# Loading a page of cached values as 64 partitions of two neighbouring rows

## The reference, cut to what matters

```python
PAST_LEN = 4096; PAGE_SIZE = 128; N_HEADS = 8; HEAD_DIM = 64; DEC_BATCH = 8; DEC_SEQ = 8
...
    past = cache_k[layer, page_table[:, :cb * ppb]].astype(f32)      # all 32 pages of each sequence
    kmean = past.reshape(B, cb, MOBA_BLOCK, N_HEADS, HEAD_DIM).mean(axis=2)
    gate = jnp.einsum('bhqd,bnhd->bhqn', qh, kmean)
    _, sel = lax.top_k(gate, ktop)                                   # 3 of 16 blocks
...
    ks = cache_k[layer, phys, :, hi5]; vs = cache_v[layer, phys, :, hi5]
    p = jax.nn.softmax(jnp.concatenate([scores on ks, scores on the new keys], axis=-1), axis=-1)
    out = einsum('bhqs,bhsd->bhqd', p, values)
```

## Time and profile before

| | us |
|---|---|
| median of 3 runs | 1244.21 (1242.72 to 1245.54) |
| span of the profiled execution, first to last instruction | 1238.5 |
| SyncE stage of loads in the batch stage, first key page to last value page issued | 121.6 to 542 |
| experts | about 670 to 1205 |

### The profile page before, as it was taken

How to read it: one execution, slowest core, us unless ns; L and a number is a source line. 1 busy time by engine, 2 the same in 40 slices (tenths; PEclk the granted TensorE clock), 3 DMA queues, 4 the chain that set the end, 5 groups by cost and what they waited for, 6 DMA issues and landing times.

```text
span 1238.5 us, 19550 instructions
## 1 busy us (share of the span) xinstructions
PE 973.8 (79%) x6934; PEld 489.3 (40%) x6934; DVE 312.2 (25%) x704; ACT 324.4 (26%) x971; POOL 104.6 (8%) x171
## 2 busy tenths in 40 slices
PE   5867976999986887889974987877777787787782
PEld 2322342535342352444443544434444343444442
DVE  1023312463715636540254000000000000000005
ACT  3021241637355555550141111011101111101101
POOL 0000000300000000000001111111111111111110
PEclk9677988999997987979976998889888989888995
DMA  9999999679879999998052999999999999999987
GB/s 341 387 387 318 369 273 335 245 270 367 312 267 374 349 383 349 326 387 311 1 203 103 366 397 396 396 394 395 397 397 397 393 395 397 396 396 394 395 330 237
DMA packets 210556, 418.65 MB, mean 338 GB/s; under 512 B 26513, under 2 KB 31250, under 8 KB 210514
## 3 DMA queue, kind: packets, MB, share of 16 engines
q1 hardware_dynamic: 193394, 395.05, 87.1%
q0 software_dynamic: 5424, 17.57, 3.7%
q10 hardware_dynamic: 11696, 5.50, 1.8%
HBM read 402.33 MB, written 15.74 MB: 338 GB/s over the span
## 4 chain that ended last, share of the span: by engine, by line
SPq 42%; PE 33%; DMA 14%; DVE 5%; issue 3%; ACT 3%; ACTq 0%; DVEq 0%; POOLq 0%; POOL 0%
SPq L326 36%; PE bank L1251 5%; PE bank L1298 4%; PE bank L1180 4%; DMA ring<-in_w_ada 3%; SPq L281 3%; PE bank L1172 3%; PE bank L1200 2%; PE bank L1254 2%; PE bank L1378 2%; DMA out_poolT<-uxr 2%; DMA ring<-in_w_up 2%; DMA ring<-in_kT 2%; DMA ring<-in_w_in 2%; PE bank L1129 1%
## 5 line engine op out<-in xcount | busy, mean ns | idle before, releaser
L1378 PE MATMUL bank<-ring,big 128*64 128x256 f32 x2048 | 280.3, 436 | 77.2 <-DMA ring<-in_w_gate 38.8
L1378 PEld LDWEIGHTS bank<-ring,big 128*64 128x64 f32 x2048 | 171.4, 157 | 198.4 <-issue 66.7
L1399 PE MATMUL bank<-ring,big 128*64 128x512 f32 x512 | 116.9, 599 | 15.5 <-ACT big L735 15.5
L733 ACT ACTIVATE big<-bank 128x256 f32<-128x256 f32 x32 | 12.3, 384 | 436.8 <-PE bank L1378 436.8
L1172 PE MATMUL bank<-ring,part 128*32 128x512 f32 x512 | 78.0, 700 | 31.7 <-ACT big L583 20.5
L1057 DVE TENSOR_TENSOR big<-big,bank 128x256 f32<-128x256 f32 x32 | 13.5, 421 | 352.7 <-ACT big L733 352.7
L1251 PE MATMUL bank<-hP,wbuf 128*128 128x512 f32 x192 | 87.6, 610 | 0.0
L583 ACT ACTIVATE big<-bank 128x256 f32<-128x256 f32 x128 | 47.8, 379 | 144.9 <-DVE big L817 135.5
L1180 PE MATMUL bank<-ring,big 128*16 128x128 f32 x2048 | 72.6, 285 | 0.3
L601 ACT ACTIVATE big<-big,ebias 128x256 f32<-128x256 f32 x128 | 63.5, 500 | 18.0 <-DVE ebias L842 18.0
L1399 PEld LDWEIGHTS bank<-ring,big 128*64 128x64 f32 x512 | 34.4, 137 | 77.5 <-issue 54.4
(11 more groups left out here) (265 smaller groups left out, 905.4 us busy)
## 6 DMA issues: line engine op xcount, KB each, us to landing
ring<-in_kT SPq DMA_DIRECT2D x256, 256.0 KB, 5.8
ring<-in_v SPq DMA_DIRECT2D x256, 256.0 KB, 6.1
ring<-in_w_gate SPq DMA_DIRECT2D x32, 2048.0 KB, 20.7
ring<-in_w_up SPq DMA_DIRECT2D x32, 2048.0 KB, 23.8
ring<-in_w_down SPq DMA_DIRECT2D x32, 2048.0 KB, 20.9
ring<-in_w_ada SPq DMA_DIRECT2D x12, 2048.0 KB, 17.8
ring<-in_w_in SPq DMA_DIRECT2D x4, 2048.0 KB, 19.1
wbuf<-in_w_in SPq DMA_DIRECT2D x4, 2048.0 KB, 11.8
```

Source lines behind the costliest of these rows:

```text
L1378: last = pe.matmul(B[1 + w][64 * f:64 * f + 64, 0:256], xv[:, c, h, :], wv[:, k, 256 * f:256 * f + 256], start=k == 0, stop=k == KT - 1)
L1399: last = pe.matmul(B[4 + p][64 * h:64 * h + 64, :], av[:, c, f, :], wv[:, k, 512 * h:512 * h + 512], start=k == 0, stop=k == FF // 128 - 1)
```

## The change

A page's 128 rows of 512 values are viewed on the DRAM side as 64 rows of 1024 (two neighbouring rows joined, 4 KB). An even page goes to partitions 0 to 63 of a pair of tiles, an odd page to partitions 64 to 127 of the same pair. A pair of tiles then holds the same two pages as before, with row 2m of a page in the first tile and row 2m + 1 in the second. The number of DMAs (one for each page), their bytes (256 KB), and where and when they are issued stay as they were. So do the instructions of every engine and their order: in the built program only the form of the value loads differs, 64 x 1024 where 128 x 512 stood. The transposes take every second column of 256 (256 columns cover two pages), starting at 0 for the first tile of a pair and at 1 for the second, so they read `L` with a step of 8 bytes. The matmuls of L1180 and the view `vslot` that they read are unchanged.

```diff
+        vpair = [ring[:, 2 * U + i * 2048:2 * U + (i + 1) * 2048].rearrange("p (g n) -> p g n", g=PPC // 2)
+                 for i in range(8)]
...
                     for g, pg in enumerate(at_):
-                        sp.dma_start(vslot[c][:, g, :], d["v"][ds(pg, 1), :, :].rearrange("a p n -> (a p) n"))\
+                        r = 64 * (g % 2)
+                        sp.dma_start(vpair[c][r:r + 64, g // 2, :], d["v"][ds(pg, 1), :, :].rearrange("a p n -> (a p) n"))\
                             .then_inc(v_full[c], 16)
...
                     for t in range(4):
-                        a = (4 * g + t) * 128
-                        last = pe.transpose(B[g % 2][:, 128 * t:128 * t + 128], L[:, a:a + 128], C["ident"])
+                        a = 4 * g * 128 + t // 2 * 256
+                        keys = L[:, a:a + 256].rearrange("p (m a) -> p a m", a=2)[:, t % 2, :]
+                        last = pe.transpose(B[g % 2][:, 128 * t:128 * t + 128], keys, C["ident"])
...
-        "v": a["cache_v"][0].reshape(nph, PAGE, AW),
+        "v": a["cache_v"][0].reshape(nph, PAGE // 2, 2 * AW),
```

## The result

The changed kernel takes 1317.35 us (median of 4 runs, 1301.93 to 1320.22), the kernel before 1243.47 us (4 runs). The ratio is 1.0568, with a 95% interval of 1.0511 to 1.0624: 74 us slower. The forecast was 1319.

What follows compares the result with a forecast made beforehand. No engine is full for a whole batch; hand-overs between key loads, scores and value work bound it. 31 us late by b = 4 plus 44 us in b = 5 to 7 gave 1244 + 75 = 1319 us, range 1242 to 1370.

Steps and rivals of the forecast that it cites:

- Two of its signs: Value phases of b = 4 to 7 near 200 GB/s; weight loads of L1200 keeping 157 ns.
- my sum: Batch stage, delays followed along the chain with 40.5 us of values a batch: 75 us more.
- the price of a page: Value loads: half of 414, 207 GB/s, or 40.5 us for a batch's values.
- the row of 180 GB/s: Profile row at the end of the returning expert loads: 180 GB/s, taken as the no-overlap bound for value loads.
- The two returning loads of 64 rows: Last two of ten returning loads, 64 x 4 KB each; claimed to show half a path, 0.43 of 422.
- half rate: Value loads: engines all on one half, then all on the other; 207 GB/s, 1319 us, chance 0.5.
- partial overlap: Rival for the value loads: pages of both halves written at once, 280 GB/s, 1268 us, chance 0.2.
- 46.6 us a batch: Value loads at the no-overlap bound of 180 GB/s; the sum gave 122 us more, 1366.
- my formula of 14.8 + values + 6.8: Period of b = 5 to 7: first to last key chunk, values, then next first chunk; 62.1 us.
- the 19 ahead of them: Weights of b = 3 land at 327.5 instead of 308.4 us, 19 us late, all on the chain.
- bounds of 0 and 40 us: Strided weight loads of the 256 transposes: nothing, or a doubling, 40 us at most; nothing was taken.
- The cover that I named: Batch stage: the longer waits hide the transposes too, also if they are slower.

Runs made afterwards that it cites:

- e5: Changed kernel with even pages on partitions 0, 2, 4 ... 126 and odd pages on 1, 3 ... 127: 1241.17 us, ratio 1.0 to the kernel before.
- e1: Changed kernel with four pages to the lower half, then four to the upper, over two chunks freed and waited for together: 1364.38 us, ratio 1.1011.
- e10: Kernel before with the changed loads and transposes for b = 4 to 7 only: 1277.24 us, ratio 1.0295.
- e9: Kernel before with the changed loads and transposes for b = 0 to 3 only: 1279.03 us, ratio 1.029.
- e8: Changed kernel without ScalarE's four stores of the samples' pooling state after b = 0: 1307.53 us.
- e11: Kernel before without ScalarE's four stores of the samples' pooling state after b = 0: 1222.15 us.
- e6: Kernel before with the strided transposes and nothing else: 1241.99 us, ratio 1.0018.
- e7: Changed kernel with the contiguous transposes of before: 1312.91 us, ratio 1.0574.
- e3: Changed kernel with each of a page's 64 partitions filled by two rows of 2 KB instead of one of 4 KB: 1318.32 us, ratio 1.062.

## Why the prediction was right, and where its working was not

The forecast of 1319 met 1317, by the mechanism that it named: TensorE waits for values, the rate is low at a busy share of 1, the landing takes 11.0 us, the stage ends 75 us later. Two of its signs failed: the rate is 255 and not near 200, and the weight loads of L1200 didn't keep their 157 ns. And that the total came within 2 us is luck: with the 33 us that a batch's values really take, my sum gives 37 us, half of what was measured. Errors went opposite ways: the price of a page was too high, and the waits that late loads bring on were too few.

**The step from the row of 180 GB/s to the mechanism held.** The two returning loads of 64 rows were the right analogue, and e5 shows the right reading of them: not half as many rows, but half of the partition range.

**The price of a page was mis-sized.** I took half of 414, 207 GB/s, since all engines would be on the same half at the same time. That is the price of one half alone, 211 in e1. What I had at nothing is the overlap of neighbouring pages: measured are 255, so 33 us for a batch's values and not 40.5, and with less alternation the rate falls (230 and 223 with longer runs). My two cases, half rate and partial overlap, were ends of one scale, and what came is between them.

By the rule of the Trainium skill's page "DMA: Bandwidth & Descriptors", section "Rules for kernel authors", that two such transfers serialize, no order of the pages should matter. The runs of this case don't bear that out: alternating pages move at 255, runs of four at 223.

Two smaller slips: with 46.6 us a batch the same sum gives 118 us and not 122, as each of seven value phases adds 6.1; and SyncE's issue time did move, from 18.7 to 23.0 us for 32 pages, which e5 shows to cost nothing here.

**The loop, b = 4 to 7.** With 33 us, my formula of 14.8 + values + 6.8 gives 54.6 us a period; 57.7 and 58.5 were measured. The last term held in b = 5: from the values of the last chunk at 514.18 to the next first chunk at 520.96 are 6.8 us. The first did not: in b = 5 the last key chunk is scored from 480.99,

```profile
480.99 1.07 PE L1175 MATMUL bank<-ring,part 128*32 128x512 f32 x8 [3.44 <-DMA ring<-in_kT]
```

which is 17.7 us after the first at 463.3, not 14.8. The batch's first key chunks themselves stood behind late values: the last of those landed at 456.4 us, and 32 key pages at 387 GB/s need 21.7 us from there, an estimate that ends at 478. The sum gave 56 us for these four batches (75 less the 19 ahead of them), and would have given 26 with 33 us of values; measured are 35 (e10) to 41 (trace).

**The first four batches were under-priced.** The sum gave 19 us, and would have given 11 with 33 us of values; e9 measured 37. Steps are missing in it, all of them to be read in the trace.

The first is in b = 1. ScalarE issues the four stores after b = 0, and TensorE waits for it before the third and fourth key chunks of b = 1:

```profile
194.45 3.64 PE L1175 MATMUL bank<-ring,part 128*32 128x512 f32 x16 [12.51 <-ACT big L586]
```

SyncE in turn waits for the scored chunks, so the values of b = 1 are issued from 203.74 us instead of 190.91 (196.14 in e10, where b = 1 is loaded as before), and the rate just before is 103 GB/s:

```profile
196.00:204.00 8.00, 8.00 (x26) 3.02 (x19) 1.38 (x2) 0.84 (x4) 0.00 (x0) 0.84 0.94 103
```

With 33 us of values my sum has the weights of b = 2 in at 245, ahead of TensorE; they came at 264.5. This step can't be laid to the stores alone, since the change costs no less without them (e8, e11).

So the weights of b = 2 come late, as forecast, and by 12 us instead of 8. In order of time, TensorE in the changed kernel:

```profile
264.50 10.00 PE L1255 MATMUL bank<-hP,wbuf 128*128 128x512 f32 x16 [7.64 <-DMA wbuf<-in_w_in]
274.43 1.92 PE L1175 MATMUL bank<-ring,part 128*32 128x512 f32 x16
```

I had stopped there and let the queue run on. But the third and fourth key chunks of b = 2 are scored only after this projection tile, and SyncE waits for `k_used` before it loads further keys. So the queue runs dry: of the stretch 269 to 272.5 us the profile gives

```profile
269.00:272.50 3.50, 3.50 (x8) 1.55 (x7) 0.00 (x0) 0.00 (x0) 0.00 (x0) 0.81 0.00 2
```

2 GB/s, where the kernel before moved 386 at that time. Here a load that is late to TensorE delays what frees the next load's slot, and the bottleneck resource itself stands idle. The values of b = 2 are issued from 280.46 instead of 265.38, 15 us late, before their own 11 us more.

After the 7.6 us of waiting TensorE's granted clock is lower, 0.81 in this stretch, a mean between its two levels of 0.50 and 1.00, and the tile took 10.0 us; undisturbed ones take 7.1. I had said that this would add a little; it is 3 us here, inside the 15, and 2 us at the first tile of b = 3, which waited 9.75 us and took 9.1.

The last step is a DMA on another queue. ScalarE's load of `w_pool` is issued in the value phase of b = 3 and takes 15.70 us to land, before 9.02:

```profile
319.63 14.86 DMA wbuf<-in_w_in
...
370.92 15.70 DMA hP<-in_w_pool
```

and TensorE stands for it, 10.5 us instead of 4.0. In e9, where the values of b = 3 are loaded as in the changed kernel, it takes 15.9 us to land, and in e10, where they are not, 9.2. So the slow transfers slow this one too, though ScalarE issued it. The 15 us at the values of b = 2, their own 11, the 2 of the tile and these 6.5 make the 35 us of the trace.

**The transposes** I costed at nothing, inside bounds of 0 and 40 us. They cost 53 ns each on average, 14 us of weight loads; as a loss of time about 2 us by e6 and not measurable in the changed kernel. The cover that I named, the waits for values, may be there, but no run shows it: e7 is too coarse.

The Trainium skill, page "SBUF — State Buffer", section "Door 1: The DMA port swizzle", would have made the step of two free; the rows of this case say 209 ns against 141 (medians).

**What settles and what doesn't.** That it is the half of the partition range is shown (e1 to e5), and so is the split of the loss between the two parts of the stage, within 6 us (e9, e10). How much of e9's 37 us each of the steps has is read from the trace and was not tried one by one. Why 16 engines that write to one half get about half the rate, no run here shows.

The Trainium skill, page "SBUF — State Buffer", section "Door 1: The DMA port swizzle", names as the cause that each half reaches only 8 of 16 ports. The rates of this case agree with it: 211 GB/s on one half, 408 to 414 on all partitions.

## What to carry to other kernels

A load that filled partitions 0 to 63 or 64 to 127 took 1.5 times as long here when the halves alternated (255 against 387 GB/s) and nearly twice on one half alone (211 against 408), while the DMA engines looked full. So compare the GB/s under the busy row, and look in your own trace for a DMA of the new shape, even a lone one at the end, before you change 256 of them. If the data force 64 rows, spread them over the whole range (every second partition) rather than over one half; what reads them must then follow that layout, which e5 leaves out. If they must be halves, alternate them. When you sum a late load forward, follow it through the waits that free the slots of later loads: the loads after it may stop altogether.

## What the runs showed of the hardware that I had not expected

- A value load as 64 x 1024 takes SyncE longer to issue than one as 128 x 512: 468 ns (median) against 333; with two rows of 2 KB for each partition (e3) 599 ns. At 0.73 us a page with all around it this became the pace of the loads in e5.
- One half of the partitions alone takes 211 GB/s. Pages on alternating halves overlap in part: 255, against 230 in runs of two and 223 in runs of four.
- A float32 weight load of 128 x 128 with a step of 8 bytes takes 209 ns (median), contiguous 141.
- 4 KB rows on all partitions, in DMAs of 512 KB and 2 MB, move at 408 to 422 GB/s, 2 KB rows in DMAs of 256 KB and 2 MB at 387.
- ScalarE's load of `w_pool` (256 KB) lands 15.7 us after its issue where the value loads in flight go to one half each, and 9.0 us in the kernel before.
